# Feed-forward of a two-layer trunk: sums and low parts of W1's operands on VectorE, squares on ScalarE, GpSimd out of the blocks

## The reference, cut to what matters

```python
D_MODEL = 1024; SEQ = 1024; DEPTH = 2; D_FF = 4 * D_MODEL
for i in range(DEPTH):
    ...                       # mixer: pooling and gating in layer 0, gated convolution in layer 1
    x = layer_norm(DEEPNORM_ALPHA * x + mix, ln1_g[i], ln1_b[i])
    hid = jnp.square(jax.nn.relu(jnp.einsum('bsd,df->bsf', x, ffn_w1[i])))
    x = layer_norm(DEEPNORM_ALPHA * x + jnp.einsum('bsf,fd->bsd', hid, ffn_w2[i]), ln2_g[i], ln2_b[i])
    gate = jax.nn.sigmoid(jnp.einsum('bsd,de->bse', x, ple_gate_w[i]))
    x = x + gate * jnp.einsum('bsk,kd->bsd', p[i], ple_w[i])
```

## Time and profile before

| | |
|---|---|
| three runs | 2245.88, 2247.32, 2248.32 us (median 2247.32) |
| the profiled execution | 2246.98 us, of which the profile's span is 2245.3 us |
| busy: TensorE, VectorE, GpSimd, ScalarE | 95%, 70%, 52%, 29% of the span |
| mean granted TensorE clock | 0.986 of full speed |
| layer 0: first trip to turn; layer 1 | from about 324 to 615 us; from about 1489 to 1780 us |

### The profile page before, as it was taken

The page is one execution under the profiler, slowest core; times in us unless marked ns, Lnnn a source line. Parts: engine busy times, 40 slices in busy tenths (PEclk is TensorE's granted clock), DMA queues, the critical chain, the costliest instruction groups (busy, mean ns, idle before and its releaser), DMA issues. The chain is left out here.

```text
span 2245.3 us, 27874 instructions
## 1 busy us (share of the span) xinstructions
PE 2142.3 (95%) x10581; PEld 1810.4 (81%) x10581; DVE 1567.9 (70%) x2065; ACT 661.0 (29%) x989; POOL 1178.1 (52%) x627
## 2 busy tenths in 40 slices
PE   8999989999979999999999999989999889999999
PEld 8877767778858888889888888777778768888899
DVE  4844788898887778665553353689888877778564
ACT  3112443222333333331211101532223233333421
POOL 4212167888677776122322222188887677776030
PEclk9999999999989999999999999999999999999999
DMA  5111013444553433111121111023444455442112
GB/s 175 38 57 55 21 62 132 141 146 155 178 201 138 172 124 130 61 48 43 38 64 50 56 38 57 20 91 139 146 142 154 164 197 177 133 169 90 38 52 76
DMA packets 150017, 233.87 MB, mean 104 GB/s; under 512 B 11168, under 2 KB 80892, under 8 KB 149884
## 3 DMA queue, kind: packets, MB, share of 16 engines
q1 hardware_dynamic: 149184, 231.78, 30.4%
q10 hardware_dynamic: 700, 0.31, 0.1%
HBM read 172.28 MB, written 59.77 MB: 103 GB/s over the span
## 5 line engine op out<-in xcount | busy, mean ns | idle before, releaser
L865 POOL TENSOR_TENSOR w_lo<-raw,w_hi 128x512 fp32r<-128x512 f32 x160 | 234.2, 1496 | 726.7 <-ACT w_hi L972 726.5
L897 POOL TENSOR_TENSOR hop_lo<-h_raw,hop_hi 128x1024 fp32r<-128x1024 f32 x106 | 294.0, 2791 | 35.4 <-ACT hop_hi L1059 35.4
L1605 PE MATMUL bank_a<-xt_hi,w_hi 128*128 128x512 f32 x640 | 251.3, 393 | 4.3 <-DVE xt_lo L1195 4.1
L1607 PE MATMUL bank_a<-xt_hi,w_lo 128*128 128x512 f32 x640 | 249.2, 389 | 0.0
L1606 PE MATMUL bank_a<-xt_lo,w_hi 128*128 128x512 f32 x640 | 249.1, 389 | 0.0
L880 POOL TENSOR_TENSOR op_lo<-op_sum,op_hi 128x512 fp32r<-128x512 f32 x112 | 182.3, 1639 | 45.2 <-ACT op_hi L1089 40.8
L1605 PE MATMUL bank_b<-w_hi,xt_hi 128*128 128x256 f32 x640 | 185.0, 289 | 13.5 <-DVE shared L1583 10.1
L902 POOL TENSOR_TENSOR wop_lo<-w_sum,wop_hi 128x1024 fp32r<-128x1024 f32 x56 | 136.9, 2444 | 113.9 <-ACT wop_hi L1065 113.9
L1605 PE MATMUL bank_b<-wop_hi,hop_hi 128*128 128x512 f32 x464 | 182.4, 393 | 13.6 <-DVE h_tile1b L1289 11.7
L1605 PE MATMUL bank_a<-wop_hi,hop_hi 128*128 128x512 f32 x448 | 178.2, 398 | 12.7 <-DVE resid L1376 12.7
L1606 PE MATMUL bank_b<-w_lo,xt_hi 128*128 128x256 f32 x640 | 183.4, 287 | 0.0
(11 more groups left out here) (175 smaller groups left out, 5371.6 us busy)
## 6 DMA issues: line engine op xcount, KB each, us to landing
h_raw<-h_spill SPq DMA_DIRECT2D x106, 512.0 KB, 3.6
h_spill<-h_tile SPq DMA_DIRECT2D x198, 256.0 KB, 2.0
w_raw<-in_ffn_w_dram SPq DMA_DIRECT2D x64, 512.0 KB, 5.7
w_raw<-in_ffn_w_dram SPq DMA_DIRECT2D x112, 256.0 KB, 3.5
raw<-in_od_w_in_dram SPq DMA_DIRECT2D x48, 256.0 KB, 2.8
raw<-in_ple_gate_w_dram SPq DMA_DIRECT2D x32, 256.0 KB, 3.1
raw<-in_ev_w_in_dram SPq DMA_DIRECT2D x24, 256.0 KB, 3.0
resid<-in_x_dram SPq DMA_DIRECT2D x8, 512.0 KB, 9.0
```

Source lines behind the costliest of these rows:

```text
L865: pool.tensor_tensor(w_lo[slab % 2][:, s], raw[:, n % NRAW, :], w_hi[slab % 2][:, s].bitcast(F32), ALU.subtract).then_inc(lo_split, 1)
L897: pool.tensor_tensor(hop_lo[k][:, :, :], h_raw[a.load(i)[0]][:, :, :], hop_hi[k][:, :, :].bitcast(F32), ALU.subtract).then_inc(ahead_pool, 1)
L1605: pe.matmul(dst, s_hi, m_hi, start=first, stop=False, skip_group_check=on_top)
L1607: return pe.matmul(dst, s_lo, m_hi, start=False, stop=last, skip_group_check=on_top)
```

## The change

In the blocks GpSimd is left with the residual's additions. VectorE makes all four sums of W1's quarters and all seven low parts (`operand_low`), and no squares. ScalarE makes ReLU and Square as two instructions on each quarter, and in the plain blocks too. The copy of c22 (L1105) goes: VectorE adds S1's bank to c21 directly. The sums h1 to h4 wait for ScalarE's squares. The residual's tiles are scaled in halves of 128x512, 1, 2 and 1 in three blocks in turn. The low part of t4 goes to GpSimd.

At the turn, the sums h1, h2, h3 of the last block are made after c21's bank is evicted (`sums_of_hid` in step A22), and SyncE loads the hidden values of the fifth and sixth product (`load_ahead` 4 and 5) ahead of the last spills and no longer behind them.

```diff
+    HID = dict(S1=("s15",), A22=("c21", "h4"), S2=("u1",), S4=("c12",), S3=("c22", "h1", "h2", "h3"))
+    HID_LAST = dict(HID, A22=("c21", "h1", "h2", "h3", "h4"), S3=("c22",))
...
                         if op == "S3":
-                            sp.wait_ge(hid_step, tr.hid[b, "q22"])
+                            if b == last:
+                                load_ahead(layer, 4)
+                            sp.wait_ge(squares_made, tr.quarter[b, "c22"])
+                            if b < last:
+                                spill_sums()
+                            else:
+                                load_ahead(layer, 5)
                         if op == "A22":
-                            sp.wait_ge(hid_step, tr.hid[b, "q21"])
+                            sp.wait_ge(squares_made, tr.quarter[b, "c21"])
                             spill(layer, b, 1, h_tile1[b % 2])
+                            if b == last:
+                                spill_sums()
...
-                if st.kind == "step":
-                    tr, j = trips[st.layer], st.item + OP_LEAD
-                    if j < len(tr.seq):
-                                .then_inc(sum_by_pool, 1)
-                            pool.wait_ge(sum_by_pool, tr.sum_pool[b, "S2"])
-                            operand_low(tr, b, "S1")
-                        elif op != "S1":
-                            operand_low(tr, b, op)
...
+                        h = h_tile[role][:, :]
+                        act.activation(h, src, ACT.Relu).then_inc(act_value, 1)
+                        act.wait_ge(act_value, st.aval_at + k + 1)
+                        act.activation(h, h, ACT.Square).then_inc(plain_squared, 1)
...
+                        def square(t):
+
+                            n = tr.quarter[b, tr.QUARTER[op]]
+                            act.wait_ge(rectified, n)
+                            act.activation(t, t, ACT.Square).then_inc(squares_made, 1)
...
+                        if op == "S4":
+                            act.wait_ge(hid_step, tr.hid[b, "c12"])
+                            act.activation(c12, c12, ACT.Relu).then_inc(rectified, 1)
+                            square(c12)
+                        if op == "S3":
+                            act.wait_ge(hid_step, tr.hid[b, "c22"])
+                            act.activation(c22, c22, ACT.Relu).then_inc(rectified, 1)
+                            square(c22)
+                        if op == "A22":
+                            act.wait_ge(hid_step, tr.hid[b, "c21"])
+                            act.activation(c21, c21, ACT.Relu).then_inc(rectified, 1)
+                            square(c21)
...
+            def operand_low(tr, b, op):
+                s = tr.index[b, op] % OPERANDS
+                src = by_four(op_sum[s]) if op[0] == "S" else w1_quarter(b, op)
+                dve.wait_ge(op_high, tr.hi[b, op])
+                dve.tensor_tensor(by_four(op_lo[s]), src, by_four(op_hi[s]).bitcast(F32), ALU.subtract)\
+                    .then_inc(op_low, 1)
...
-
-                        dve.wait_ge(act_value, st.aval_at + k + 1)
-                        t = h_tile[2 * st.half + k][:, :]
-                        dve.tensor_tensor(t, t, t, ALU.mult).then_inc(dve_value, 1)
...
+                    if 0 < j <= len(tr.seq) and tr.seq[j - 1][1] not in ("S1", "S2"):
+                        operand_low(tr, *tr.seq[j - 1])
+                    if j < len(tr.seq) and tr.seq[j][1][0] == "S":
...
+                        if op == "S2":
+                            dve.wait_ge(w1_summed, tr.summed[b, "S1"])
+                            dve.tensor_tensor(dst, by_four(op_sum[tr.index[b, "S1"] % OPERANDS]),
+                                              w1_quarter(b, "A11"), ALU.subtract).then_inc(w1_summed, 1)
+                            dve.wait_ge(w1_summed, tr.summed[b, "S2"])
+                            operand_low(tr, b, "S1")
+                        if op == "S4":
+                            dve.tensor_tensor(dst, w1_quarter(b, "A12"),
+                                              by_four(op_sum[tr.index[b, "S2"] % OPERANDS]), ALU.subtract)\
+                                .then_inc(w1_summed, 1)
+                            dve.wait_ge(w1_summed, tr.summed[b, "S4"])
+                            operand_low(tr, b, "S2")
...
+                        def sums_of_hid():
+                            sum_free(4)
+                            dve.wait_ge(squares_made, tr.quarter[b, "c22"])
+                            dve.tensor_tensor(h1, c12, c22, ALU.add).then_inc(hid_step, 1)
+                            sum_free(5)
+                            dve.wait_ge(hid_step, tr.hid[b, "h1"])
+                            dve.tensor_tensor(h2, h1, c11, ALU.subtract).then_inc(hid_step, 1)
+                            dve.wait_ge(hid_step, tr.hid[b, "h2"])
+                            dve.tensor_tensor(c12, c11, c12, ALU.subtract).then_inc(hid_step, 1)
...
                         if op == "S1":
-                            dve.wait_ge(part_moved, tr.move[b, "s5"])
-                            dve.tensor_tensor(c22, c22, c21, ALU.add).then_inc(hid_step, 1)
+                            dve.wait_ge(spill_out[3], a.spilled(3, b - 1))
+                            dve.wait_ge(part_moved, tr.move[b])
+                            dve.wait_ge(trip_done, tr.done[b, op])
+                            dve.tensor_tensor(c22, c21, bank, ALU.add).then_inc(hid_step, 1)
...
-                            squared_relu(c21, "q21", "c21")
+                            if b == FFN_BLOCKS - 1:
+                                sums_of_hid()
+                            sum_free(6)
+                            dve.wait_ge(squares_made, tr.quarter[b, "c21"])
+                            dve.wait_ge(hid_step, tr.hid[b, "h2"])
                             dve.tensor_tensor(h4, c21, h2, ALU.subtract).then_inc(hid_step, 1)
...
-                            squared_relu(c12, "q12", "c12")
                         if op == "S3":
                             dve.tensor_tensor(c22, c22, bank, ALU.add).then_inc(hid_step, 1)
-                            squared_relu(c22, "q22", "c22")
+                            if b < FFN_BLOCKS - 1:
+                                sums_of_hid()
...
-                        dve.tensor_tensor(r, r, gb_rows[:, 0, :], ALU.mult).then_inc(gained, 1)
+                        dve.tensor_tensor(resid[:, t, c], resid[:, t, c], gb_rows[:, 0, c], ALU.mult)\
+                            .then_inc(gained, 1)
...
-                        pe.wait_ge(part_moved, tr.move[b, "s5"])
+                        pe.wait_ge(hid_step, tr.hid[b, "s15"])
```

187 lines of the change are left out of this document (63 added, 124 removed).

## The result

The changed kernel takes 2225.08 us (median of 4 runs, 2224.16 to 2225.89), the kernel before in the same session 2247.82 us (2245.88 to 2248.77). The ratio is 0.99, with a 95% interval of 0.9883 to 0.9917. So it is faster, but by less than half of what I forecast, and outside the range of 2183 to 2213 us.

A forecast was written before the change was run, and what follows sets the result against it. TensorE, busy 2142.3 of 2245.3 us, bounds the kernel, so only its gaps can be won: 2246.98 - 23 (blocks) - 18 (entry) - 10.4 (turn) = 2195.6, forecast 2195 us; 8 in 10 within 2183 to 2213.

The forecast's parts named there:

- The blocks: Strassen blocks: the 16 waits at S1 for op_lo go, block period 20.53 to 19.04 us; 23 us saved, bounds 10 and 24.
- the walk along the deadlines: In a block, from S3's end: VectorE's evictions, sums and low parts followed in its queue, all found ready in time.
- 1.8 us to spare: S2's low part in a block: ready 6.4 us after S3's end, wanted at 8.16.
- two stalls behind ScalarE: VectorE waits for ReLU and Square behind c22's and c21's eviction: 1.4 us each, 2.8 in a block.
- 16 half-tile additions in 12 blocks: All that GpSimd still does in the blocks; VectorE's instructions there were priced as without contention, 0.68 us.
- the floor: Strassen blocks: a trip is 2.72 us, so a block costs 19.04 us if nothing is late.
- The third rival: Each block: a new wait, c22's spill or S2's low part, replaces the old; blocks give nothing, 2218 us; chance 0.07.
- The entry: S2's first trip, once a layer: its gap nearly closes, 9.1 us saved per layer, 18 us, bounds 12 and 18.6.
- Nothing else changes: Outside blocks, entry and turn: no further effect on the time, put at 0 us.
- The turn: Last block to W2's products: earlier c21 eviction and loads save 10.4 us for both layers, bounds 0 and about 34.
- The claim that the later gaps hang on the loads landing: Turn: TensorE's later restarts follow h4, spills and loads of hidden values; this chain starts 5.2 us earlier per layer.
- The rival of VectorE's queue as the bound: Each block: two stalls and 15 SBUF instructions at 1.03 us make 22.6 us, total about 2295; slower had chance 0.05.

The follow-up runs named there:

- run 2: Changed kernel without GpSimd's 16 half-tile bias additions to the residual in each layer's feed-forward, so it computes something else: 2205.31 us.
- run 3: Changed kernel with ScalarE's Square of c11 moved behind the high part of A22: 2208.37 us.
- run 4: Changed kernel with the residual's bias additions on VectorE behind its multiplications, GpSimd idle in the blocks: 2209.51 us.
- run 8: Changed kernel with VectorE's sums of x behind w_lo, Square of c11 behind A22's high part, and bias additions on VectorE: 2190.63 us.
- run 1: Changed kernel with one more VectorE wait: its six sums of x start only after GpSimd's four w_lo low parts: 2212.44 us.
- run 7: Changed kernel with the squares of the two plain blocks back on VectorE: 2223.29 us.
- run 5: Changed kernel with the turn's order undone: h1 to h3 ahead of c21's eviction, the two loads behind the spills: 2233.43 us.
- run 12: Run 8's kernel with VectorE's additions ahead of preparation in every product of W2 from the fourth on: 2182.44 us.
- run 11: Run 8's kernel with VectorE's additions of the fourth to sixth product of W2 ahead of the preparation before each: 2188.9 us.

## Why the prediction was wrong

**The blocks: this step failed.** It is the walk along the deadlines, with GpSimd's 16 additions put at nothing. The deadlines of the prediction let S1's low part be ready "at about 0.0" against 2.72, and gave S2's low part "1.8 us to spare". In a block with one half it went as follows, on TensorE (the first trip after S3) and VectorE (low parts of A22 and S1, c22's eviction, S2's low part):

```profile
1697.90 0.39 PE L1603 MATMUL bank_a<-xt_hi,op_hi 128*128 128x512 f32 x1
...
1697.78 0.69 DVE L1188 TENSOR_TENSOR op_lo<-w_raw,op_hi 128x512 fp32r<-128x512 f32 x1 [1.70 <-ACT op_hi L1059]
...
1699.10 0.69 DVE L1188 TENSOR_TENSOR op_lo<-op_sum,op_hi 128x512 fp32r<-128x512 f32 x1
1699.71 0.68 DVE L1319 TENSOR_TENSOR h_tile<-h_tile,bank_b 128x512 f32<-128x512 f32 x1
...
1705.28 0.69 DVE L1188 TENSOR_TENSOR op_lo<-op_sum,op_hi 128x512 fp32r<-128x512 f32 x1
```

After S3's end (1697.90) S1's low part was there at 1.9, c22's eviction at 2.5 (forecast 0.8), S2's low part at 8.1 (forecast 6.4, wanted at 8.16). All of it is shifted by the wait of 1.70 that the first VectorE row shows. I counted two stalls behind ScalarE and walked only from VectorE's side; the third lies in ScalarE's own order, where A22's high part stands behind ReLU and Square of c11. The two that I counted were sized right: 1.42 to 1.43 us measured, 1.4 forecast; so were VectorE's own instructions, 0.68 to 0.69. And I took "16 half-tile additions in 12 blocks" for harmless, in the same text that shows what one GpSimd instruction does to VectorE: each cost 1.1 us on the instruction beside it, which here carried the chain to ScalarE and back. In a block with two of them S1's low part was there 3.6 us after S3's end, against 2.72. The spare time that was to cover both did not exist. Runs 2, 3 and 4 each take one charge away and win back 16.5, 13.8 and 12.0 of the 18.2 us that the blocks lack to the floor, far more together than there was to win, as it is when several charges share one spare time. With them mended (run 8) first A12 to first product is 511.4 us. The forecast was 534.4 - 23 = 511.4. So the floor was right, and the claim that the change reaches it was wrong. The third rival, a new wait in each block, had a chance of 0.07: it had one of the two places, S2's low part, but neither S1's nor the cause, and gave the blocks nothing where they gave 4.8.

**The entry: right where I looked, wrong in what I left out.** S2's first gap closed for 19.4 us against 18 forecast and a bound of 18.6. The bound was twice layer 1's loss of 9.3 us; layer 0 had lost 10.1. The prediction followed what the squares' removal does to what comes after, and not what was running beside them: the sums moved forward onto `w_lo`, whose last piece TensorE needed. The prediction's "Nothing else changes" put this at nothing; it cost 13.2 us, and runs 1 and 7 show it from two sides. By the rule of the Trainium skill, "SBUF — State Buffer", section "Who interferes with whom", the engine that issues first holds the pair of ports and the other blocks. The trace agrees that one side alone pays: VectorE's sums ran at 1.17 us each, and GpSimd took 13.35 us for four that took 6.61 with the sums held back. But GpSimd's first subtraction stood through eight VectorE instructions in a row, where the rule speaks of one. The prediction read the rule for VectorE's losses alone.

**The turn: right in mechanism, small in size.** 14.0 us against 10.4, bounds 0 to 34. By run 5 the order makes 12.5 of them. The eviction of c21 was done 11.7 us after the first product's start, forecast 14.0, since ScalarE's high part was there after 7.1 us and not 8.2, and VectorE's low part took 1.6 us and not 2.6. So the second product had no wait where 1 us was forecast, h4 came 6.0 us earlier than before and not 3.7, and the five loads were issued 6.6 us earlier and not 5.2. The claim that the later gaps hang on the loads landing is not borne out after the change: run 12 left the loads alone and took 10.7 us out of the same stretch by VectorE's order. In layer 1 of runs 8 and 12 the five loads are issued 18.2 and 18.3 us after the first product, and the seventh product starts 41.3 and 37.0 us after it. What held the seventh product in the changed kernel was that its bank was freed late, behind two contended sums of 3.3 us.

**The rest.** No table loads were added (five before and after); ScalarE's 112 us more lay beside TensorE but for Square of c11. The rival of VectorE's queue as the bound was nearer than I thought: the blocks with one half were full to within 0.1 us, which I had put at 1.7 to spare. Its sum has a small slip, on which nothing rests: at 0.93 us an instruction the block is 21.05 us and not 20.9.

Left open: why run 5's median moved 4 us less than its stretch, why run 1's profiled execution is 5.7 us shorter outside the changed part, why the medians of runs 2, 3 and 4 fell by some 3 us more than their blocks did, and how much of run 11's new gap is ScalarE's order and how much contention. Putting the turn's preparation on another engine wasn't tried.

## What to carry to other kernels

Follow a deadline round the whole loop of engines, in each one's queue order, and not only down the queue that got more work: the stall that used up this block stood in the queue of the helper. When work is taken off an engine, list what was running beside the removed instructions, since what follows moves forward and meets it; a deliberate wait there can be worth as much as the work moved away (12.6 us for one line). And where two engines slow each other, a few left-over instructions on the slower one can cost more than the same work on the busy one (here 15.6 us).

## Not expected of the hardware

- A GpSimd addition of a half tile took 1.69 us on average and put 1.1 us on one VectorE instruction; VectorE's additions from PSUM in the turn took 2.47 us for four also between 1781 and 1812 us, where GpSimd was never idle.
- Four identical GpSimd subtractions took 6.61, 8.50 or 13.35 us, by what VectorE had queued beside them; in the last case the first alone took 9.68, while VectorE's sums took 1.17 us each beside it.
- ReLU and Square on 128x512 in place took 0.63 us each on ScalarE, 1.43 us as a pair seen from VectorE; the one fused instruction on VectorE took 0.69.
